# Stationary weights, tokens moving, for the roped projections of a sparse-attention decoder block

## What is computed

```python
xn = rmsnorm(h, norm_mix[layer])
z = xn @ w_in[layer]
(q_a, kc, vc, ksl, vsl, kwn, vwn, g_a, q_b, k_b, v_b, iq, ik, iw, g_merge) = jnp.split(z, offsets, axis=-1)
q_a = rope(q_a.reshape(b, s, NSA_HEADS, HEAD_DIM), positions)
kc = rope(kvh(kc), positions)
ksl = rope(kvh(ksl), positions)
kwn = rope(kvh(kwn), positions)
...
q_b = rope(q_b.reshape(b, s, DSA_HEADS, HEAD_DIM), positions)
# rope, for the two halves x1, x2 of a head of 64:
return jnp.concatenate([x1 * cos - x2 * sin, x1 * sin + x2 * cos], axis=-1)
# the indexer (dsa_mixer)
score = jnp.einsum('bqh,bqhs->bqs', iw_c, jax.nn.relu(idx_logits))
_, sel = lax.top_k(score, topk)
```

## Time and profile before

| | |
|---|---|
| median of 3 runs | 1657.48 us (1656.28 to 1658.52) |
| profiled execution, its span | 1655.2 us (no other time of this execution is given) |
| PE busy | 1599.1 us, 97% of the span |
| DVE, ACT, POOL busy | 1208.3, 686.8, 619.4 us |
| DMA traffic | 172 MB, mean 104 GB/s |

### The profile page before, as it was taken

The page is one execution under the profiler, slowest core; times in us unless marked ns, Lnnn a source line. Parts: engine busy times, 40 slices in busy tenths (PEclk is TensorE's granted clock), DMA queues, the critical chain, the costliest instruction groups (busy, mean ns, idle before and its releaser), DMA issues.

```text
span 1655.2 us, 25363 instructions
## 1 busy us (share of the span) xinstructions
PE 1599.1 (97%) x9216; PEld 1349.7 (82%) x9216; DVE 1208.3 (73%) x2143; ACT 686.8 (41%) x1381; POOL 619.4 (37%) x438
## 2 busy tenths in 40 slices
PE   6899999999999989999999998999999999999997
PEld 5778888888879978899877876888888888887885
DVE  6877877999964757877666157776666776667978
ACT  5644443212185657766521034322222222344445
POOL 4234244222061133633222117454444444445454
PEclk9999999999999989999999999999999999999999
DMA  6013243522162110010063441233333334474533
GB/s 197 14 51 117 86 118 111 173 84 93 45 167 81 74 47 20 27 40 27 16 189 127 127 153 46 88 116 112 98 95 96 96 96 172 146 272 159 158 105 121
DMA packets 153691, 172.19 MB, mean 104 GB/s; under 512 B 19552, under 2 KB 103520, under 8 KB 153312
## 3 DMA queue, kind: packets, MB, share of 16 engines
q1 hardware_dynamic: 153568, 170.57, 32.3%
HBM read 121.00 MB, written 49.55 MB: 103 GB/s over the span
## 4 chain that ended last, share of the span: by engine, by line
PE 53%; DMA 2%; DVE 2%; issue 1%; POOL 0%; ACT 0%; SPq 0%; DVEq 0%; ACTq 0%
PE psA L1579 9%; PE psA L1580 9%; PE psA L1581 9%; PE psT L1581 6%; PE psT L1580 6%; PE psT L1579 6%; PE psT L1586 3%; PE psT L1787 3%; DMA wd<-in_w_down_dram 2%; PE psA L1673 1%; PE psA L1674 1%; DVE h L2400 0%; DMA s<-scratch_gates 0%; POOL w_lo L398 0%; DVE h L2384 0%
## 5 line engine op out<-in xcount | busy, mean ns | idle before, releaser
L398 POOL TENSOR_TENSOR w_lo<-w_raw,w_hi 128x1024 fp32r<-128x1024 f32 (+2 forms) x52 | 120.7, 2325 | 242.2 <-ACT w_hi L393 242.2
L1175 POOL TENSOR_TENSOR w_lo<-w_sum,w_hi 128x1024 fp32r<-128x1024 f32 x44 | 116.5, 2650 | 121.9 <-ACT w_hi L1464 121.9
L1401 ACT ACTIVATE s<-s,nmax 128x640 f32<-128x640 f32 (+7 forms) x192 | 144.0, 752 | 29.7 <-DVE nmax L2254 28.3
L1198 POOL TENSOR_TENSOR w_lo<-act_raw,w_hi 128x512 fp32r<-128x512 f32 x77 | 108.0, 1404 | 105.4 <-ACT w_hi L1492 105.4
L1579 PE MATMUL psA<-w_hi,xTh 128*128 128x512 f32 (+2 forms) x320 | 120.7, 377 | 5.0 <-POOL w_lo L398 3.4
L1586 PE MATMUL psT<-ident,s 128*128 128x128 f32 x816 | 120.4, 277 | 0.8 <-ACT s L1401 0.8
L1581 PE MATMUL psA<-w_hi,xTl 128*128 128x512 f32 (+2 forms) x320 | 117.7, 368 | 0.0
L1580 PE MATMUL psA<-w_lo,xTh 128*128 128x512 f32 (+2 forms) x320 | 117.7, 368 | 0.0
L2344 DVE COPY pT<-psT 128x512 f32<-128x512 f32 (+1 forms) x116 | 69.7, 600 | 53.6 <-PE psT L1586 53.5
L1586 PEld LDWEIGHTS psT<-ident,s 128*128 128x128 f32 x816 | 94.2, 141 | 17.1 <-issue 7.4
L2475 DVE TENSOR_TENSOR w_lo<-wd,w_hi 128x512 fp32r<-128x512 f32 x77 | 90.4, 1178 | 23.8 <-ACT w_hi L1499 23.6
(11 more groups left out here) (372 smaller groups left out, 4730.6 us busy)
## 6 DMA issues: line engine op xcount, KB each, us to landing
act_raw<-scratch_act SPq DMA_DIRECT2D x77, 256.0 KB, 3.0
w_raw<-in_w_in_dram SPq DMA_DIRECT2D x28, 512.0 KB, 4.0
scratch_act<-act SPq DMA_DIRECT2D x33, 256.0 KB, 2.1
scratch_act<-act_sum SPq DMA_DIRECT2D x33, 256.0 KB, 2.1
wd<-in_w_down_dram SPq DMA_DIRECT2D x33, 256.0 KB, 3.0
scratch_gates<-gate_out SPq DMA_DIRECT2D x32, 256.0 KB, 3.0
gates<-scratch_gates SPq DMA_DIRECT2D x30, 256.0 KB, 4.2
a<-in_w_gate_dram SPq DMA_DIRECT2D x22, 256.0 KB, 3.3
```

Of the source, the lines that this page charges most:

```text
L398: nc.gpsimd.tensor_tensor(self.lo[n % RING][:, 0:u], self.raw[n % RAW][:, 0:u], self.hi[n % RING][:, 0:u].bitcast(F32), ALU.subtract).then ...
L1175: nc.gpsimd.tensor_tensor(lo2[n % RING][:], block_of(n)[:], hi2[n % RING][:].bitcast(F32), ALU.subtract)\
L1198: nc.gpsimd.tensor_tensor(lo2[slot][:, 0:512], act_raw[n % 6][:], hi2[slot][:, 0:512].bitcast(F32), ALU.subtract)\
L1401: a_.activation(s_sb[v % SR][:, 0:n], s_sb[v % SR][:, 0:n], ACT.Exp, scale=-1.0, bias=nmax[:, BR[a], i, h:h + 1], accum_out=psum_p[:, BR[a ...
```

## The change

The roped queries, keys and the compressed inputs are projected as the gates are: weights stationary, 512 tokens moving, so that z comes out turned. There are six groups (`TILES`): two of DSA queries, one of `kc` and `ksl`, one of `vc` and `kwn`, two of NSA queries. Each has 256 columns, two weight items of 512 KB (`part` 0 and 1, four channel blocks each), two token halves `m` and two PSUM banks `t` for each half. A pair (group, half) is called a unit; there are 12. The weights' columns are permuted on the way through `split_hi` and `split_lo` (`views`), so that bank 0 holds the first halves of the heads and bank 1 the second. DVE makes four products with turned tables (`tile_rope`), POOL two sums and two lo parts (`tile_sums`), ACT the two hi parts (`tile_hi`), and SP writes four pieces of 256 KB (`spill`). What isn't roped or turned (`vsl`, `vwn`, the NSA gates; 280 columns) is projected in eight steps `nat_step` with tokens stationary, which stand between the indexer's units: two early ones, then six, each followed by up to three units (`late_units`). Seven counts stand ahead of each `tile_rope`. The gate steps use eight PSUM banks in place of four. Queries are read back by four DMAs of 32 partitions instead of one, keys by 16 instead of two.

```diff
-    ORDER = [IDX, QB, CMP, WKV, QA]
-    COLS = {IDX: (o_kb, o_gm - o_kb), QB: (o_qb, 512), CMP: (o_kc, 512), WKV: (o_kwn, 280), QA: (0, 512)}
+    NAT = [(o_vsl, P, 0), (o_vwn, P + 3 * H, P)]
+    TILES = [("dsa", 0), ("dsa", 1), ("ks", 0), ("vw", 0), ("nsa", 0), ("nsa", 1)]
...
+        for n in range(N_NAT + 2, N_TILE + 2):
+            w1.load(sp, n)
+        for g in range(len(TILES)):
+            w1.load(sp, N_TILE + 2 * g + 2)
+            if g:
+                spill(2 * g - 1)
+            w1.load(sp, N_TILE + 2 * g + 3)
+            spill(2 * g)
+        w1.load(sp, N_GATE + 2)
+        spill(2 * len(TILES) - 1)
...
+        def tile_sums(n):
+            g, m = tile_units[n]
+            kind, t = TILES[g][0], tm[n % 2]
...
+                for r, op in enumerate((ALU.subtract, ALU.add)):
+                    pool.wait_ge(rope_done, NT + 2 * n + r + 1)
+                    nc.gpsimd.tensor_tensor(t[2 * r][:], t[2 * r][:], t[2 * r + 1][:], op).then_inc(cos_done, 1)
...
+                pool.wait_ge(bh_done, NT + piece_no[n, r])
...
             if q == NT - 1:
-                for n in (5, 6, 7):
+                for n in range(N_NAT, N_TILE):
                     w1.split_lo(pool, n)
-        w1.split_lo(pool, NCH + 3)
+        for n in range(N_TILE, N_TILE + 2):
+            w1.split_lo(pool, n)
+        for g in range(len(TILES)):
+            w1.split_lo(pool, N_TILE + 2 * g + 2)
+            if g:
+                tile_sums(2 * g - 1)
+            w1.split_lo(pool, N_TILE + 2 * g + 3)
+            tile_sums(2 * g)
+        tile_sums(2 * len(TILES) - 1)
...
                 z_evac(k - 1)
-                for n in split_at(k - 1)[1]:
-                    w1.split_hi(act, n)
+                if k - 1 == NT - 1:
+                    for n in range(N_NAT, N_TILE):
+                        w1.split_hi(act, n)
             if 0 <= k - 2 < NT:
                 block_hi(k - 2)
...
+        def nat_step(j):
+            if j < 4:
+                pe.wait_ge(sc_done, EARLY - 3 + j)
...
+        def tile_group(g):
+            for part in range(2):
+                n = N_TILE + 2 * g + part
+                pe.wait_ge(w1.lo_done, n + 1)
...
+                for m in range(2):
+                    if part == 0:
+                        tile_free(g, m)
+                    half = slice(HALF * m, HALF * (m + 1))
+                    for t in range(2):
+                        mm = three(tile_bank(g, m, t),
...
-            if EARLY <= v < EARLY + 2:
-                pe.wait_ge(sc_done, EARLY - 2 + 2 * (v - EARLY))
-            elif v >= 4 and not EARLY + 2 <= v < EARLY + 4:
+            if v >= EARLY + 2:
+                pe.wait_ge(sc_done, v - 1)
+            elif 4 <= v < EARLY:
                 pe.wait_ge(sc_done, v - 3)
...
-        for v in range(EARLY, len(iunits)):
-            id_unit(v)
-        stage2(NT, Z_STEPS)
+        for j in range(N_EARLY, NT):
+            nat_step(j)
+            for v in late_units(j):
+                id_unit(v)
+        for g in range(len(TILES)):
+            tile_group(g)
...
+        def tile_rope(n):
...
+            for p in set_before(n):
+                dve.wait_ge(bl_done, NT + p)
+            dve.wait_ge(z_ps, tile_sum(g, m, 1))
...
+            v_.tensor_tensor(t[0][:], x1, cos, ALU.mult)
+            v_.tensor_tensor(t[1][:], x2, sin, ALU.mult).then_inc(rope_done, 1)
+            v_.tensor_tensor(t[2][:], x2, cos, ALU.mult)
+            v_.tensor_tensor(t[3][:], x1, sin, ALU.mult).then_inc(rope_done, 1)
...
+        for n in range(len(tile_units)):
+            some_counts(IN_UNIT)
+            tile_rope(n)
         some_counts(PASSES)
         selection()
...
-            sp.dma_start(qt[k % 2][:].rearrange("p h t -> p (h t)").bitcast(F32), qD[set_][i])\
-                .then_inc(q_in[k % 2], 16)
+            for c in range(4):
+                sp.dma_start(qt[k % 2][32 * c:32 * (c + 1), :, :].bitcast(F32), qD[set_][i, c].rearrange("(h e) t -> e h t", h=H))\
+                    .then_inc(q_in[k % 2], 16)
```

More of the change, by code:

```diff
@@ L142, in hybrid_block @@
     raw1, hi1, lo1 = ring_memory(one, "w1")
[L143 to L149, removed]
+    with ExitStack() as s:
+        zs = [sb(s, f"z{n}", [P, 512]) for n in range(2)]
+        rot = sb(s, "rotated", [P, 512])
+        ro = [sb(s, f"roped{n}", [P, 512]) for n in range(2)]
+        blk = [sb(s, f"blocks{n}", [P, 8, P], F32R) for n in range(3)]
+        cosT = sb(s, "cosT", [P, NT, HD])
+        sinT = sb(s, "sinT", [P, NT, HD])
+    tm = [[sb(one, f"turn_part{n}{r}", [P, HALF]) for r in range(4)] for n in range(2)]
+    th1 = [[sb(one, f"turned_hi{n}{r}", [P, HALF], F32R) for r in range(2)] for n in range(2)]
+    tl1 = [[sb(one, f"turned_lo{n}{r}", [P, HALF], F32R) for r in range(2)] for n in range(2)]
     with ExitStack() as s:
@@ L291, in chunk_items @@
     def chunk_items(src, first, width):
[L292 to L296, removed]
+        return [[(src[:, 2 * n:2 * n + 2, first:first + width], 0, 2, width, width, 0)] for n in range(KT // 2)]
+    items1 = chunk_items(w_in, *IDX_COLS)
+    N_NAT = len(items1)
+    items1 += [[(w_in[:, 2 * n:2 * n + 2, c:c + w], 0, 2, w, NAT_W, at) for c, w, at in NAT] for n in range(KT // 2)]
+    N_TILE = len(items1)
+    for key in TILES:
+        for n in range(2):
+            rows = slice(4 * n, 4 * n + 4)
+            if key[0] == "vw":
+                parts = [(w_in[:, rows, o_vc:o_vc + P], 0, 4, P, P, 0)]
+                parts += [(w_in[:, rows, o_kwn + 32 * c:o_kwn + 32 * (c + 1)], 512, 4, 32, P, 64 * (c % 2) + 32 * (c // 2))
+                          for c in range(4)]
+            else:
+                at, parts = 0, []
+                for c, w in TILE_COLS[key]:
+                    parts.append((w_in[:, rows, c:c + w], 0, 4, w, 256, at))
+                    at += w
+            items1.append(parts)
+    N_GATE = len(items1)
+    PAIRS = {N_TILE + 2 * g + n for g, key in enumerate(TILES) for n in range(2) if key[0] != "vw"}
+    items1 += [[(w_in[:, :, o_gm + P * j:o_gm + P * (j + 1)], 0, KT, P, P, 0)] for j in range(2 * KT)]
     wa = A["w_branch_nsa"][0].rearrange("(k p) c -> p k c", p=P)
@@ L383, in load @@
                 sp.wait_ge(self.lo_done, n - RAW + 1)
[L384 to L386 removed]
+            for src, at, k, w, row, first in self.items[n]:
+                dst = self.raw[n % RAW][:, at:at + k * row].rearrange("p (k w) -> p k w", k=k)
+                sp.dma_start(dst[:, :, first:first + w], src).then_inc(self.raw_in[n % RAW], 16)
         def split_hi(self, act, n):
@@ L2171, in some_counts @@
                 one_count(n)
-        for q in range(NT, Z_STEPS + 1):
-            if q < Z_STEPS:
-                rope(q)
-            if q > NT:
-                block_lo(q - 1)
-            if q < Z_STEPS and q not in PAIRED:
-                c, i = zsteps[q]
-                some_counts(BEHIND_PAIR[c] if i == 1 else 2 if i == NT - 1 else IN_STEP[c])
+        for n in range(len(tile_units)):
+            some_counts(IN_UNIT)
+            tile_rope(n)
         some_counts(PASSES)
```

459 lines of the change are left out of this document (231 added, 228 removed).

## The result

The changed kernel takes 1685.8 us (median of 4 runs, 1681.61 to 1688.06) against 1658.0 for the kernel before in the same comparison: ratio 1.016, 95% interval 1.0139 to 1.0181. It is 27.8 us slower. The forecast was 1662 in a range of 1646 to 1675: the direction was right, the size far too small, and the time lies outside the range. The profiled execution took 1688.06, the slowest of the four, and its span is 1686.3, 31.1 more than before.

A forecast was written before the change was run, and what follows sets the result against it. PE and DVE were taken to bound the front. Front −16.6, weights +17, clock +1.5 and reads +2.5 made +4.4 on the span of 1655.2, or 1659.6; the runs' median is 2.3 above, so 1662, range 1646 to 1675.

The forecast's parts named there:

- front without stalls: From the start to the gates' end: transposes go, the indexer's start grows, gates end at 437.1 in place of 453.7, −16.6.
- weights in the tiles: Tile items: weights come every 13.35 us against PE's 10.88, items 13 and 14 arrive late, +17; bounds 4 to above 30.
- clock behind the last gap: Gates' end: PE's clock falls in idle gaps, the last being 3 to 5 us, +1.5 (between 0 and 3).
- attention's reads: Attention: more DMA issues per query tile and for the keys lengthen PE's query waits, +2.5 (bounds 0 to 5).
- two engines bound the front: Up to attention's start: PE and DVE both bound it, so only a change that relieves both can shorten it.
- The start: Indexer before the tiles: seventh z_turn near 80.8, third nat_step near 86.2, first tile matmul at 132.4.
- POOL's sums and lo parts at 1.30 us: Tiles: POOL's operations keep 1.30 us; the rival that they take 1.53 was worth +10, 1672, chance .10.
- The serial lap: Tiles: one load, ACT hi, POOL lo, four POOL operations and a spill issue in series, 13.35 us against PE's 10.88.
- T0: Time of the first tile matmul, forecast at 132.4 us.
- the rival of slow narrow reads: Attention: reads into 32 partitions flow half as fast, 6 us of PE idle at query tile 7, +8, 1670, chance .25.
- What the page doesn't put down to an engine is PE's own sequencer: Profile page: the chain that ended last is 53% PE, nothing else above 2%; the rest was read as PE's sequencer.
- the 26.1 us: PE's time for transposes from 82.12 to 453.7, taken as 26 groups of up to eight; the change removes them, −26.

The follow-up runs named there:

- late_spills: Changed kernel with each weight load of the tiles put ahead of one more unit's spills in SP's queue: 1660.75 us, ratio to the kernel before 1.0007.
- the wide reads: Changed kernel with each query tile and each key table read by one DMA of 128 partitions, attention's values not the reference's: 1668.85 us, ratio 1.0053.
- all nine profiles: Profiles of the changed kernel and the eight runs built on it; the DVE operation near 1027 us took 2.38 to 2.41 us.
- the other twelve kernels: The follow-up kernels: eight built on the changed kernel, four on the kernel before; measured from 1643.92 to 1676.18 us.

## Why the prediction was wrong

The terms of the sum, as forecast and as measured (us):

| term | forecast | measured | from |
|---|---|---|---|
| front without stalls | −16.6 | −16.9; −15.6 in the changed kernel's execution | late_spills; its first tile matmul at 133.24 |
| weights in the tiles | +17 | +21.7 | start of item 14 |
| clock behind the last gap | +1.5 | +2.4 | last sigmoid, 462.23 |
| attention's reads | +2.5 | +15.0 (17.0 by the wide reads) | lag at 463 and at 600 us |
| the collision at 1027 | none | +3.7 | lag before and behind it |

The measured terms make −15.6 + 21.7 + 2.4 + 15.0 + 3.7 = 27.2, beside a difference of the medians of 27.8.

**Right.** That two engines bound the front, and that the change takes DVE out of it: DVE idles 24.7 us before the attention. The front without stalls. The start: z_turn, nat_step and first tile matmul each within .9 us. POOL's sums and lo parts at 1.30 us. The serial lap as a mechanism, with its place and its members: load 4 was issued at T0 + 23.6 (forecast 23.4), the lap was 13.9 (13.35), and the longest wait, 5.77, stood at the third gate item, as written. The waits before it were not the 2 to 3 us each of the forecast: .53, 4.01, .82, .90, 2.44 and .74.

**Wrong, first and largest: the choice between the attention's two prices.** The sum took "+2.5 with a small wait at tile 3", the issues alone, since no row showed a narrow DMA; the rival of slow narrow reads had .25 and a price of +8. The runs settle it for the rival: narrow reads alone cost 14.3 in the kernel before, wide ones give back 17.0 in the changed one. The rival's mechanism was right in place (query tile 7 behind the keys, 7.55 us of idle; forecast 6) and too small again: 11.6 us of waits became 15.0 us of delay by 600 us. What the other 3.4 consist of was not measured. The Trainium skill, "SBUF — State Buffer", section "Door 1: The DMA port swizzle", spoke for this rival, and the issues' price had nothing behind it but the absence of a row. With the rival in the sum it would have been 1670.

**Wrong, second: the size of the lap's loss.** "+17 in all" was 21.7. The lo of item 4 came at T0 + 33.1, not 31.0, since its load landed in 5.2 us and not in the median 3.9 of the earlier trace rows. The nine laps to item 13 took 123.9 instead of 122.4, with landings of 4.5 to 5.1 in the last four loads, and item 14 came 17.0 behind item 13 instead of about 16. The mechanism stands and the landing was mis-sized; 21.7 lies within the bounds given from the earlier trace rows. The step "The last gaps here are 3 to 5 us: +1.5 (between 0 and 3)" was off by 1 us only: slow stretches behind inner gaps are taken out of the next wait. The price there was taken from one group of transposes.

**Not in the sum: 3.7 us at 1027.** No term of the forecast was for code behind the attention. There DVE, .35 us later than before against POOL, met a POOL operation in all nine profiles. Of the profiled 31.1 us another 3.9 are left: 1.2 between 600 and 990 us, −1.0 between the collision and 1460, and 3.7 between 1460 and 1520. In the last stretch the other twelve kernels shift by −.4 to 2.6 us against the kernel before, whether they are built on it or on the changed one. So these steps are not shown to be the change's own; and the profiled execution was 2.3 us above its median.

**Two readings of the prediction that don't hold.** "What the page doesn't put down to an engine is PE's own sequencer": the shares of part 4 add up to 58% because the chain begins at 679 us, so it doesn't bear on the front, and the reading of PE as the front's bound rests on the windows alone. And the transposes before were 208 in 32 groups of 8, 6, 4 and 8, not in 26; they equal 26 groups of eight, and the 26.1 us were what was left of a measured stretch, so the sum isn't touched.

## What to carry to other kernels

In a queue that both feeds and drains (here SP: loads and spills), put each load ahead of the drain that its predecessor's consumer delays; a chain load, hi, lo, drain, load is a lap, and it must be under the pace of the engine it feeds. When a layout change splits a transfer, look at which partitions each piece touches before counting the pieces: here pieces of neighbouring partitions cost 14 us, and the number of DMAs 1, which is within the noise. Where such a lap is slower than PE, read PE's lateness from the lap and add what the slow clock loses behind the last gap; what it loses behind the others comes off the next wait. Expect a later part of the program to shift by a few us when the times of its engines move against each other by less than one.

## What was not expected of the hardware

Eight DMAs of 32 neighbouring partitions landed a 2 MB table with a median of 11.1 us, eight of 32 partitions taken one in four with 5.1, and four of 64 neighbours with 15.6 (512 KB each). After a wait of 4.0 us PE ran with starts .43 us apart for 5.1 us (225.42 to 230.55) before it was back at .23; after one of 2.44 us it first ran at .23 for 1.6 us and then at .43 for 3.4 (278.26 to 281.62). A DVE operation on two columns took 2.40 us, with the POOL operation beside it, in place of .17.
